# One-hot matrices of an expert gate, built token by token with per-row scalars instead of three broadcast passes

## The reference, cut to what matters

```python
s1 = einsum('thc,kc->thk', q[..., :half], keys1)
s2 = einsum('thc,kc->thk', q[..., half:], keys2)
v1, i1 = top_k(s1, 16)
v2, i2 = top_k(s2, 16)
cand = (v1[..., :, None] + v2[..., None, :]).reshape(..., 256)
sc, ci = top_k(cand, 16)
eid = take(i1, ci // 16) * 128 + take(i2, ci % 16)
gate = softmax(sc, -1)
hid = gelu(einsum('td,thkd->thk', x, expert_u[eid]))
out = einsum('thk,thkd->td', gate * hid, expert_v[eid])
```

## Time and profile before

| | |
|---|---|
| median of 3 runs | 2220.26 us (2219.65 to 2227.92) |
| the profiled execution | 2228.68 us |
| its span, first to last instruction | 2226.6 us |
| the 48 octets on VectorE, first start to last start | 1316.6 to 1639.1 us |
| `phase_combine` begins | about 1662.8 us |
| mean granted TensorE clock | 0.969 |

### The profile page before, as it was taken

The page is one execution under the profiler, slowest core; times in us unless marked ns, Lnnn a source line. Parts: engine busy times, 40 slices in busy tenths (PEclk is TensorE's granted clock), DMA queues, the critical chain, the costliest instruction groups (busy, mean ns, idle before and its releaser), DMA issues. The chain is left out here.

```text
span 2226.6 us, 33908 instructions
## 1 busy us (share of the span) xinstructions
PE 2109.9 (95%) x12934; PEld 1910.4 (86%) x12934; DVE 1641.7 (74%) x3051; ACT 773.2 (35%) x1237; POOL 569.1 (26%) x354
## 2 busy tenths in 40 slices
PE   8997987979999989999999999999989999999998
PEld 7997877977965689999999999999987787778776
DVE  5634637666234332699999979999988888898898
ACT  4334332232233132222224434444443333333332
POOL 0000014000000000021211215555546655675530
PEclk9998778999999999999999999999999999999999
DMA  5223210023244040267765848989889999999993
GB/s 162 84 89 110 72 54 1 8 88 138 77 170 170 22 136 17 100 234 250 271 230 196 278 148 334 337 334 335 333 340 381 388 388 387 383 384 388 379 375 122
DMA packets 223216, 483.75 MB, mean 217 GB/s; under 512 B 12015, under 2 KB 137199, under 8 KB 221446
## 3 DMA queue, kind: packets, MB, share of 16 engines
q1 hardware_dynamic: 177030, 314.56, 39.8%
q0 software_dynamic: 46080, 167.79, 20.8%
HBM read 423.29 MB, written 58.36 MB: 216 GB/s over the span
## 5 line engine op out<-in xcount | busy, mean ns | idle before, releaser
L2873 PE MATMUL ps<-v_high_low,gated_high_low 128*128 128x512 f32 x2304 | 535.1, 393 | 22.6 <-ACT gated_high_low L2941 17.6
L2873 PEld LDWEIGHTS ps<-v_high_low,gated_high_low 128*128 128x128 f32 x2304 | 434.7, 190 | 122.8 <-ACT v_high_low L2939 20.6
L2477 PE MATMUL ps<-x_high_low,u_high_low 128*128 128x384 f32 x1024 | 355.6, 347 | 0.2 <-ACT u_high_low L2543 0.2
L2478 PE MATMUL ps<-x_high_low,u_high_low 128*128 128x384 f32 x1024 | 345.0, 337 | 0.0
L2965 POOL DMA_INDIRECT outputs<-peer_v,kept x138 | 256.7, 1860 | 170.4 <-DVE kept L2982 137.6
L2594 POOL DMA_INDIRECT scores<-peer_u,kept x64 | 94.1, 1470 | 781.6 <-DVE kept L2714 604.7
L2482 PE MATMUL ps<-x_high_low,u_high_low 128*128 128x384 f32 x1024 | 204.7, 341 | 0.0
L2552 ACT ACTIVATE kept<-ps 128x384 f32<-128x384 f32 x128 | 62.9, 491 | 406.4 <-PE ps L2482 400.0
L2477 PEld LDWEIGHTS ps<-x_high_low,u_high_low 128*128 128x128 f32 x1024 | 192.5, 188 | 0.5 <-ACT u_high_low L2543 0.5
L2478 PEld LDWEIGHTS ps<-x_high_low,u_high_low 128*128 128x128 f32 x1024 | 192.8, 188 | 0.0
L3045 DVE TENSOR_TENSOR v_high_low<-raw_v,v_high_low 128x1024 fp32r<-128x1024 f32 x120 | 146.4, 1220 | 52.9 <-ACT v_high_low L2939 52.9
(11 more groups left out here) (453 smaller groups left out, 4295.3 us busy)
## 6 DMA issues: line engine op xcount, KB each, us to landing
experts<-peer_u SPq DMA_DIRECT2D x63, 1024.0 KB
raw_v<-peer_v SPq DMA_DIRECT2D x60, 1024.0 KB
hidden<-kept SPq DMA_DIRECT2D x64, 384.0 KB
gates<-scores SPq DMA_DIRECT2D x12, 2048.0 KB
first_hidden<-hidden SPq DMA_DIRECT2D x16, 768.0 KB, 18.7
outputs<-gates SPq DMA_DIRECT2D x16, 768.0 KB
outputs<-hidden SPq DMA_DIRECT2D x16, 768.0 KB
first_gates<-gates SPq DMA_DIRECT2D x15, 768.0 KB
```

The lines of the kernel that those rows point to most:

```text
L2477: pe.matmul(o, utr[:, b, HI, k], xr[:, HI, k, 0:DN], start=(k == 0), stop=False)
L2478: pe.matmul(o, utr[:, b, HI, k], xr[:, LO, k, 0:DN], start=False, stop=False)
L2873: ins = pe.matmul(bank(c, 2 * t + h), gr[:, slot, x, DN * b + P * t:DN * b + P * t + P], vr[:, slot, y, D * b + 512 * h:D * b + 512 * h + ...
```

## The change

Before, three instructions build an octet's matrices. Each covers 128 partitions x 8 tokens x 128 keys, and both keys and gates are tensors that are broadcast along the key dimension. After, each token gets two instructions of 128 x 128 elements. They read `iota` and take the key, and for the first matrix also the gate, as scalars of each row (a 128 x 1 operand). Compare and gate are one instruction, so the wait between the compare and the multiply goes, with its semaphore.

```diff
-    hot_set, hot_first, made, gkept = s("gated_one_hots_set"), s("first_one_hots_set"), s("gates_made"), s("gates_kept")
+    hot_set, made, gkept = s("gated_one_hots_set"), s("gates_made"), s("gates_kept")
...
                 after(v, made, 2 * (o - 1))
-                keys, k2 = over(iota, 1, [P, OCT, NK]), hot2[slot].rearrange("p (t k) -> p t k", t=OCT)
-                k1 = gated[slot].rearrange("p (t k) -> p t k", t=OCT)
-                v.tensor_tensor(k1, keys, over(kt[:, 0, t0:t0 + OCT], 2, [P, OCT, NK]), ALU.is_equal).then_inc(hot_first, 1)
-                v.tensor_tensor(k2, keys, over(kt[:, 1, t0:t0 + OCT], 2, [P, OCT, NK]), ALU.is_equal)
-                v.wait_ge(hot_first, o + 1)
-                v.tensor_tensor(k1, k1, over(kt[:, 3, t0:t0 + OCT], 2, [P, OCT, NK]), ALU.mult).then_inc(hot_set, 1)
+                k1, k2 = (x.rearrange("p (t k) -> p t k", t=OCT) for x in (gated[slot], hot2[slot]))
+                for t in range(OCT):
+                    key1, key2, g = (kt[:, i, t0 + t:t0 + t + 1] for i in (0, 1, 3))
+                    v.tensor_scalar(k1[:, t], iota, key1, g, ALU.is_equal, ALU.mult)
+                    ins = v.tensor_scalar(k2[:, t], iota, key2, None, ALU.is_equal)
+                ins.then_inc(hot_set, 1)
                 if lows[0] < NK:
                     low()
```

## The result

The changed kernel took 2229.52 us (median of 13 runs, 2226.75 to 2240.06), the kernel before 2220.37 us (13 runs, 2219.15 to 2229.30). The ratio is 1.0039, with a 95% interval of 1.0025 to 1.0054. The change made the kernel slower by 9 us, a small loss that is clear of the noise. The forecast was no change at 2220.

A forecast was written before the change was run, and what follows sets the result against it. The prediction took TensorE, at 6.86 us an octet, to bound the octets; VectorE's saving of 0.17 us an octet would become waiting, so 0 us in sum and 2220 us, range 2209 to 2252.

The forecast's parts named there:

- What bounds: Among the 48 octets, TensorE sets the pace at 6.86 us an octet, with VectorE's own work at 6.84.
- the 0.03 us that hid in front of L2607: VectorE's short wait per octet for ScalarE's copy before low(), hidden in overlap, taken as a sign that VectorE follows TensorE.
- One scalar: Each new 128-column VectorE instruction with one row scalar takes 288 ns, or 203 ns start to start.
- Two scalars: A second row scalar in eight VectorE instructions an octet adds nothing; upper bound 67 ns each, 0.54 us together.
- 0.19 us of room: VectorE's new octet sum of 6.67 us stays this far under TensorE's 6.86.
- the second scalar costs as much as the first: Rival: VectorE needs 7.21 us an octet, 0.35 over TensorE; 17 us slower, 2237 us; chance 0.12.
- The threshold: VectorE may take 3.44 us for an octet's one-hots, 215 ns for each of 16 instructions, before octets pass on excess.
- GpSimd: Rival: GpSimd's indirect DMAs block VectorE's new instructions among the octets; 36 to 81 us slower, 2256 to 2301; chance 0.20.
- One column at a time: Rival: the new VectorE instructions process single columns, 0.88 us an octet beyond the room; 42 us slower, 2262; chance 0.05.
- TensorE freed: Rival: VectorE held TensorE back, whose blocks could take 6.67 us; 9 us faster, 2211; chance 0.06.
- The tail: At the phase's end, VectorE's last dot products wait for their rows as before, so nothing changes.

The follow-up runs named there:

- e4: The changed kernel with the second matrix made for the first two octets only, which leaves out the others' second keys: 2220.18 us, ratio 0.9985 to the kernel before.
- e1: The changed kernel with a constant 1.0 in place of the gate scalar, which leaves the gates out: 2220.62 us, ratio 0.9986 to the kernel before.
- e3: The changed kernel with the second matrix built in one broadcast instruction as before, same result: 2219.91 us, ratio 0.9988 to the kernel before.
- e6: The changed kernel with a constant 1.0 for every second token's gate, leaving out half the gates: 2220.46 us, ratio 0.9985 to the kernel before.
- e5: The changed kernel with GpSimd gathering only the 59 row sets used before the octets: 2223.87 us, ratio 1.0003 to the kernel before.
- e2: The changed kernel with a second row scalar, a column of ones, for the second matrix too: 2255.51 us, ratio 1.0135 to the kernel before.
- e7: The changed kernel with the first matrix in two broadcast instructions as before, the second token by token: 2247.63 us, ratio 1.0091 to the kernel before.

## Why the prediction was wrong, point by point

**What bounds.** Right. TensorE sets the pace at 6.86 us in the kernel before, with VectorE 0.02 behind it. e4 shows it: with 1.6 us less for VectorE in each octet than in the changed kernel, the stretch was 319.0 us. The step on which this rested, the 0.03 us that hid in front of L2607, was the right thing to look at. One reading beside it was wrong, and did no harm: the L2607 of 1402.20 works on the copy that ScalarE made at 1401.07, which is that of the next block. By then 92 of the L2607 had started, and the L2482 of 1404.06 is only the 91st block's. TensorE needs this `low()` one block later, at about 1404.06 + 6.87 = 1410.93, so it is early by 7.5 us, not by 0.6. What VectorE can hold TensorE up with is the one-hots, and there the waits of after lie.

**One scalar.** 203 ns each were forecast, start to start; the rows of after say about 0.20 (1399.68 to 1399.88, and 0.195 in the pairs of e1). The median duration was 275 ns, for 288 forecast.

**Two scalars.** This is the step that failed: "I take nothing on top". The sum had the term with its right upper bound, 67 ns for each, and measured was 60 ns in the duration (335 against 275) and 0.055 us start to start. The bound was nearly the value. The reason that I gave for the lower end ("no row shows any cost that goes with the number of operands alone") was not a reason: the one row scalar already cost 67 ns over an immediate, and that was such a row. The nearest row spoke for the upper end. With 0.055 for eight instructions the sum is 8 x 0.255 + 8 x 0.20 + 1.14 + 2.28 = 7.06 us, 0.20 over 6.86, and 48 x 0.20 = 9.6 us, for a measured 0.18 an octet. So the forecast missed by the term that it put at nothing: VectorE did not keep 0.19 us of room but went 0.19 over. It is the rival "the second scalar costs as much as the first" with a smaller price (it said 7.21 us and 17 us). It had a chance of 0.12.

**The threshold.** The text gave the room, 215 ns for each of 16 instructions. Measured is a mean of 3.64 / 16 = 228. The excess is 3.64 - 3.44 = 0.20 us in an octet, 9.6 us over 48. e1, e3 and e4 show that below the threshold nothing is paid, and e6, which lies 0.01 us above it, pays 0.7 us.

**GpSimd.** The rival fell: 0.75 to 1.69 us in each octet were at stake. In an octet of after one L2745 (at 1399.88) shows 0.47 us in place of 0.33, and GpSimd's DMA of 1398.62 ends at 1400.31, within it. But the next instruction starts at its usual distance. e5, without any indirect DMA, has octets as far apart as after (0.01 us less). The largest delay that may be GpSimd's is the 0.07 us in the octet of e6 above. The Trainium skill (SBUF — State Buffer, on who interferes with whom) says that a VectorE instruction in a two-port mode and a GpSimd instruction block each other for the whole instruction. Here the start-to-start distance of VectorE's instructions shows no wait of an indirect DMA's length, and an indirect DMA among sixteen of them took 0.94 us in after, as long as beside the short searches (0.93 to 1.18 us in e1, e2 and e6).

**One column at a time, TensorE freed.** Both fell: 275 ns at 128 columns fits the 288 forecast and not 67 ns more, and e3 and e4 found no faster TensorE.

**The tail.** I had it unchanged. In the profiles it is not. VectorE's last dot product waits longer for its row:

```profile
1658.86 1.23 DVE L2615 SCALAR_TENSOR_TENSOR kept<-kept 128x1024 f32<-128x1024 f32 x1 [3.08 <-DMA kept<-peer_u,kept]
```

Before, that wait was 0.45 us. From the last L2506 to VectorE's last instruction of the phase it was 11.9 us before and 15.3 after. Profiles of e2, e6 and e7 show waits of 3.1, 4.1 and 2.5 us there, those of e1, e3 and e4 0.5. In the kernel before, GpSimd is done issuing that last row at 1648.13, 0.36 us ahead of the store of the gates (L2424, 1648.49); in after it is done at 1648.42, 0.39 us behind it (1648.03). The eight profiles with gathers divide the same way: before, e1, e3 and e4 are done 0.35 to 0.39 us ahead of that store and wait about 0.5 us, and after, e2, e6 and e7 are done 0.39 to 0.42 us behind it and wait 2.5 to 4.1. That the row then queues behind the store fits this and is not shown by a run.

Little of that wait reaches the time, because VectorE was not what the next phase waited for before. The first instruction of the next phase on VectorE, before and after:

```profile
1662.90 0.06 DVE L3029 MEMSET kept<- 128x1 f32 x1 [4.34 <-PEq L3091]
1663.30 0.06 DVE L3029 MEMSET kept<- 128x1 f32 x1 [1.78 <-PEq L3091]
```

VectorE stood idle for 4.34 us in front of it before and for 1.78 after. From the last L2506 of the even octets to this instruction it is 23.1 us before and 24.2 after. So 3.4 us more for VectorE made 1.1 us more for the phase. From the start of L1079 to this instruction, which leaves the lost 8 us out, it is 1345.8 us before and 1353.9 after: 8.1 us more. These 8.1 are the 8.3 of the stretch, 1.1 of the tail and 1.3 less ahead of the octets.

## What to carry to other kernels

Price an instruction by its operands and not by its columns alone: each scalar that is read for every row (a 128 x 1 operand) cost 0.055 to 0.067 us here, whether it is the first or the second, which is as much as 128 columns at the rate of this operation (128 x 0.518 ns). Where two engines are level to 0.02 us an octet, any term of that size decides, but in one direction only: a saving on the engine that follows is worth nothing, and a cost beyond the room is paid in full in every repetition. When a price is unknown between two bounds, take the bound to which a row of the trace is nearest.

## What was not expected of the hardware

The 8 us that separate executions of the same kernel go with one stretch in which TensorE's granted clock differs. The stretch from 270 to 290 us in the windows of before (the columns are the busy time and the instructions of TensorE's matmuls, its weight loads, VectorE, ScalarE and GpSimd, then the granted clock, the share of the DMA and its GB/s):

```profile
270.00:290.00 20.00, 18.56 (x105) 18.21 (x106) 6.97 (x22) 3.14 (x10) 0.00 (x0) 0.64 0.00 1
```

The same stretch of e3:

```profile
270.00:290.00 20.00, 18.90 (x160) 18.36 (x160) 8.68 (x26) 7.85 (x17) 0.00 (x0) 1.00 0.08 28
```

The clock was 0.64 in the one and 1.00 in the other (means over the stretch of two levels, 1.2 and 2.4 GHz), and TensorE got through 105 matmuls in the one and 160 in the other. In the 20 us ahead of it both were below full (0.76 and 0.83). The nine profiles divide the same way: the three that lost the 8 us (before, e2, e4) show 0.64 to 0.68 in this stretch, the six others 1.00. In the 20 us behind it, where e3 is further on in its work, it is the other way round (0.87 and 0.66). Why the clock fell in some executions and not in others is open. Once late, an execution stays late: before and e3 are 8.7 us apart at L1079 (317.1 and 308.4) and 8.9 at the end (spans of 2226.6 and 2217.7).
